# The WKV recurrence of a two-block fp32 model on one core: from one group of heads at a time to two groups in alternation

## Chip, cores and metric

One core of a Trainium2 chip runs the whole program once. The metric is the device time of that execution in microseconds, as the median of several runs.

## What is computed

The reference is two model blocks on 256 tokens of width 2048 in fp32. The first is banded attention, a multi-window pool and a gated feed-forward with a short convolution. The second has an RWKV-7 mixer, then a differential-attention layer. Only the RWKV-7 mixer's recurrence and what surrounds it are touched here:

```
def step(S, inp):
    r_t, w_t, k_t, v_t, kk_t, a_t = inp
    sa = jnp.einsum('bhvk,bhk->bhv', S, kk_t)
    S = (S * w_t[:, :, None, :]
         - sa[..., None] * (kk_t * a_t)[:, :, None, :]
         + v_t[..., None] * k_t[:, :, None, :])
    y = jnp.einsum('bhvk,bhk->bhv', S, r_t)
    return S, y
...
mu = jnp.mean(y, -1, keepdims=True)
yc = y - mu
var = jnp.mean(yc * yc, -1, keepdims=True)
y = (yc * lax.rsqrt(var + GN_EPS)).reshape(B, T, C) * gn_g + gn_b
...
y = (y + bonus.reshape(B, T, C)).astype(x.dtype)
return (y * jax.nn.silu(g)) @ w_out
```

There are 32 heads of 64 channels. y is normed per head ("head norm"), gets a bonus term, is gated, and is multiplied with the output weights (the out-projection).

## The kernel before

All engines are programmed by hand: each has its own function with its instructions in fixed order, and semaphores between them. No scheduler moves anything, so the text of each engine's function is its queue.

Large products. Every weight matrix comes in units of 4 x 128 rows by 256 columns. SP loads a unit (raw_w), ACT rounds it (w_hi), DVE subtracts (w_lo, `split_unit`, L2448), and PE multiplies both parts with the activations. The out-projection begins with `first_body` (L931, L934): 8 units, each in two halves, in four depths x. Depth x needs the k-tiles of head group x as rounded operand (`operand_hi`, ACT) and rest (`operand_lo`, DVE); the gates are counts of `gn_ready`, 4 per group.

The recurrence. The 256 tokens are cut into 4 chunks (c = 0 to 3) of 64, the 16 tiles of heads into 4 groups (g = 0 to 3) of 4 tiles, 8 heads each. The order is `STEPS = [(g, c) for g in range(4) for c in range(NCH)]`: 16 steps, all chunks of a group and then the next group. PE's function `step(n)` issues, in this order:

- `x_second`: the state's part of x (c > 0), `k_pairs(n + 1)`: products of k with r and kappa of the next step
- first u product: inverse blocks times x; `turn_v(n + 1)`
- cross product, `beta_pairs(n + 1)`, state times r into y (c > 0), second u product
- `turn_k(n + 1)`, state sums (c < 3), `turn_beta(n + 1)`, `x_first(n + 1)`, y product

All these products are small: `quads` (L1319) issues eight of 64 columns into quarters of the array. Between them ACT copies x, the first u, half of u, v and k/beta out of PSUM, and y into its place; DVE masks the pairs (`read_kappa` L3037, `read_rho` L3043), adds the cross product to x (L3057), copies the other half of u (L3063) and moves the state (L3075, L3077, L3081). POOL squares y (L866), multiplies the bonus (L849) and gates (`by_gate`, L854). SP loads for each step its inverse and cross blocks (`load_t`), three steps deep, and spreads the rows of 1/std over partitions through DRAM (`spread_rows`).

The head norm of group g-1 runs in the steps of group g: squares summed on PE (`group_squares`, L1423) in its first step, variance and reciprocal (L3060, L3096) on DVE, square root on ACT, spread by DMA, and `head_pair` (L3108, L3113) on DVE for two tiles at a time. Only group 3 is left for after the loop: `head_squares` (L1430) after unit 0 of `first_body` and `last_rows_wide` (L1439) after unit 3, which spreads the rows by products into PSUM. Weight units 0 to 3 of the out-projection are split within the steps 6, 10, 14, 14 (ACT) and 10, 14, 15, 15 (DVE), by `SPLIT_AT` and `LOW_SPLIT_AT`; at step 15 DVE does them after its copy of u and `operand_lo(0)`.

Of the kernel before, what the change touches and what calls it, by code (L numbers as in the profile page):

```python
# [14 lines left out]
P = 128  # L15
T = 256
# [130 lines left out]
def program(nc, h):  # L147
# [14 lines left out]
    with root:  # L162
# [95 lines left out]
        with ExitStack() as s1:  # L258
# [8 lines left out]
            with ExitStack() as s2:  # L267
# [7 lines left out]
                with ExitStack() as s3:  # L275
                    HTP = sb(s3, "xs_pair", [P, 2, T])
# [3 lines left out]
                    with ExitStack() as s4:  # L280
                        TB = sb(s4, "inverse_blocks", [P, 3, 4, CHUNK])
                        S = sb(s4, "wkv_s", [P, 4, CHUNK])
# [17 lines left out]
            with ExitStack() as s2:  # L300
# [4 lines left out]
                with ExitStack() as s3:  # L305
                    SMALL = sb(s3, "wkv_small", [P, 2, 8, T])
                with ExitStack() as s3:
                    sb(s3, "place_of_small", [P, 2, 8, T])
                    GSQ = sb(s3, "group_norm_squares", [P, 4, T])
                    GROWS = sb(s3, "head_rstd_rows", [P, 2, T])  # L310
                    GWIDE = sb(s3, "head_rstd_wide", [P, 4, T])
                with ExitStack() as s3:
                    sb(s3, "place_of_half_b", [P, KD, T])
                    HT3B = sb(s3, "xs_quarter_b", [P, 4, T])
# [86 lines left out]
        l_ready, ones_ready, decays = sem("log_decay"), sem("decay_ones"), sem("decays_ready")  # L401
# [4 lines left out]
        inv_in, blanked = sem("lt_loaded"), sem("blocks_blanked")  # L406
# [8 lines left out]
        x_done, xs_ready, u_done, us_ready = sem("wkv_x_done"), sem("wkv_x_ready"), sem("wkv_u_done"), sem("wkv_u_ready")  # L415
# [10 lines left out]
        dist_in, lam_prod, lam_sum, lam_exp = sem("dist_and_ln_rows_loaded"), sem("lam_products"), sem("lam_sum"), sem("lam_exp")  # L426
# [112 lines left out]
        def k_kappa(m):  # L539

            return SMALL[:, m, 0, :].rearrange("p (i c) -> p i c", i=4)

        def with_rho(m):

            return SMALL[:, m, 1:3, :].rearrange("p h (i t) -> p h i t", i=4)

        def v_and_u(m):

            return SMALL[:, m, 3:5, :].rearrange("p a b -> p (a b)").rearrange("p (j e h t) -> p j e h t", j=2, e=2, h=2)

        def k_and_beta(m):

            return SMALL[:, m, 5:7, :].rearrange("p a b -> p (a b)")

        def k_beta_turned(n):

            g, c = STEPS[n]
            return 3 * g + min(c, 2) + 1

        def v_turned(n):  # L560

            return n + 1 + (k_beta_turned(n - 1) if n else 0)
# [4 lines left out]
        v_bank = lambda n: V_BANK if n else SIDE[:, 1, T:]  # L567
        kb_bank = lambda n: KB_BANK if n else SIDE[:, 3, :]

        def by_two(x):  # L570

            return x.rearrange("p e (j t) -> p e j t", j=2)
        SPLIT_AT = [6, 10, 14, 14]
# [2870 lines left out]
```

## Time and profile before

| | us |
|---|---|
| median of 3 runs | 2164.82 |
| lowest, highest | 2163.67, 2165.35 |
| span of the profiled execution | 2162.8 |
| of it, first product of the loop to the last y product | 1467.31 to 1562.63 |

The span runs from the first to the last instruction; the runs' times also hold what lies around it, and the difference of the profiled span to the median is 2.0 us. The trace has a start and a duration for each instruction. Groups of matmuls are shown as one row with their count; each fp32 product counts as two. A start is measured, an end modelled, so lengths of small products are read from start to start.

### The profile page before, as it was taken

Reading aid. Unit: us, or ns where it says so; the run is one execution under the profiler, and the core shown is the slowest. Engines: PE = TensorE matmul, PEld = TensorE weight load, DVE = VectorE, ACT = ScalarE, POOL = GpSimd, SP = SyncE. Lnnn points to the kernel's source line nnn. Section 1 sums busy time; section 2 is a strip of 40 time slices with the busy share of each in tenths; the row PEclk is TensorE's granted clock in tenths of the full one; section 3 lists DMA queues with packets and bytes.
Section 4 is the critical chain, followed back from the end, with each engine's and each line's share of the span. In section 5 each row is a group of like instructions: output and inputs, shape, how many; then the busy total and the mean of one; then the engine's idle time right before and its main releaser. Section 6 shows DMA issues by size and latency. Waiting matters only on the chain.

```text
span 2162.8 us, 36139 instructions
## 1 busy us (share of the span) xinstructions
PE 2128.1 (98%) x13990; PEld 1808.1 (84%) x13990; DVE 1466.9 (68%) x2083; ACT 1063.6 (49%) x1516; POOL 85.8 (4%) x75
## 2 busy tenths in 40 slices
PE   9999999999999999999899999999899999999998
PEld 7888878888888888888788888887788888888886
DVE  6556568885478855786795599884776544567656
ACT  5444455444444433444644766544434534456543
POOL 0800000000000000000000000001211000000000
PEclk9999999999999999999999999999999999999999
DMA  9654545555656556555465656653454555654553
GB/s 299 202 165 157 172 160 185 190 186 189 198 185 190 187 187 199 187 180 177 150 203 167 196 183 179 206 160 86 129 174 142 185 185 195 186 155 146 173 197 117
DMA packets 398856, 384.43 MB, mean 178 GB/s; under 512 B 43660, under 2 KB 395460, under 8 KB 397764
## 3 DMA queue, kind: packets, MB, share of 16 engines
q1 hardware_dynamic: 398728, 382.66, 55.8%
q8 instruction: 88, 1.44, 0.3%
q14 instruction: 40, 0.33, 0.1%
HBM read 375.73 MB, written 6.87 MB: 177 GB/s over the span
## 4 chain that ended last, share of the span: by engine, by line
PE 89%; DVE 7%; issue 2%; ACT 1%; DMA 1%; POOL 0%; SPq 0%; DVEq 0%; ACTq 0%; POOLq 0%
PE acc L894 35%; PE acc L897 17%; PE acc L1020 5%; PE acc L1022 5%; PE acc L1021 5%; PE acc L931 3%; PE acc L986 2%; PE acc L987 2%; PE acc L988 2%; PE aux L1319 2%; PE acc L934 1%; DVE w_lo L3001 1%; PE acc L1619 1%; PE acc L1620 1%; PE acc L1621 1%
## 5 line engine op out<-in xcount | busy, mean ns | idle before, releaser
L2448 DVE TENSOR_TENSOR w_lo<-raw_w,w_hi 128x1024 fp32r<-128x1024 f32 (+1 forms) x570 | 683.5, 1224 | 438.3 <-ACT w_hi L1692 437.5
L1692 ACT ACTIVATE w_hi<-raw_w 128x1024 fp32r<-128x1024 f32 (+1 forms) x570 | 586.3, 1045 | 706.0 <-PE acc L897 413.0
L894 PE MATMUL acc<-h,w_hi 128*128 128x512 f32 x1664 | 525.8, 397 | 0.0
L897 PEld LDWEIGHTS acc<-h,w_lo 128*128 128x128 f32 x1664 | 312.6, 188 | 73.8
L897 PE MATMUL acc<-h,w_lo 128*128 128x256 f32 x1664 | 327.0, 278 | 0.0
L894 PEld LDWEIGHTS acc<-h,w_hi 128*128 128x128 f32 x1664 | 254.7, 189 | 1.0
L894 PE MATMUL acc<-x_split,w_hi 128*128 128x512 f32 x704 | 225.1, 401 | 0.0
L894 PE MATMUL acc<-xs_b,w_hi 128*128 128x512 f32 x512 | 162.0, 398 | 1.0 <-DVE w_lo L3001 0.9
L897 PEld LDWEIGHTS acc<-x_split,w_lo 128*128 128x128 f32 x704 | 132.2, 188 | 31.2
L3001 DVE TENSOR_TENSOR w_lo<-raw_w,w_hi 128x1024 fp32r<-128x1024 f32 x96 | 116.8, 1219 | 42.1 <-ACT w_hi L2165 41.2
L894 PE MATMUL acc<-xs_a,w_hi 128*128 128x512 f32 x448 | 142.3, 399 | 0.7 <-DVE w_lo L3001 0.7
L897 PE MATMUL acc<-x_split,w_lo 128*128 128x256 f32 x704 | 138.7, 278 | 0.0
L1020 PE MATMUL acc<-w_hi,ff 128*128 128x512 f32 x346 | 135.2, 391 | 2.9 <-DVE w_lo L2448 2.9
L1021 PE MATMUL acc<-w_lo,ff 128*128 128x512 f32 x352 | 137.5, 391 | 0.0
L1022 PE MATMUL acc<-w_hi,ff 128*128 128x512 f32 x346 | 135.1, 390 | 0.0
L2165 ACT ACTIVATE w_hi<-raw_w 128x1024 fp32r<-128x1024 f32 x96 | 100.8, 1054 | 53.2 <-PE acc L897 45.6
L897 PEld LDWEIGHTS acc<-xs_b,w_lo 128*128 128x128 f32 x512 | 96.2, 188 | 22.7
L894 PEld LDWEIGHTS acc<-x_split,w_hi 128*128 128x128 f32 x704 | 108.1, 189 | 2.4 <-issue 0.8
L897 PEld LDWEIGHTS acc<-xs_a,w_lo 128*128 128x128 f32 x448 | 84.2, 188 | 20.0
L897 PE MATMUL acc<-xs_b,w_lo 128*128 128x256 f32 x512 | 100.6, 278 | 0.0
L897 PE MATMUL acc<-xs_a,w_lo 128*128 128x256 f32 x448 | 88.1, 278 | 0.0
L894 PEld LDWEIGHTS acc<-xs_b,w_hi 128*128 128x128 f32 x512 | 78.0, 189 | 3.4 <-issue 1.6
(459 smaller groups left out, 3223.5 us busy)
## 6 DMA issues: line engine op xcount, KB each, us to landing
raw_w<-in_w_up SPq DMA_DIRECT2D x172, 512.0 KB, 3.5
raw_w<-in_a_w_in SPq DMA_DIRECT2D x124, 512.0 KB, 3.9
raw_w<-in_w_in SPq DMA_DIRECT2D x64, 512.0 KB, 3.9
raw_w<-in_w_down SPq DMA_DIRECT2D x64, 512.0 KB, 3.5
raw_w<-in_b_w_qg SPq DMA_DIRECT2D x64, 512.0 KB, 3.7
raw_w<-in_w_o SPq DMA_DIRECT2D x32, 512.0 KB, 3.5
raw_w<-in_a_w_out SPq DMA_DIRECT2D x32, 512.0 KB, 3.5
raw_w<-in_w_k_shared SPq DMA_DIRECT2D x32, 512.0 KB, 3.3
```

The source lines that it names most:

```text
L894: pe.matmul(ACC[2 * b + f], WHI[:, q if hi is None else hi, k, f * P:(f + 1) * P], op[:, kt, :, :].rearrange("p h t -> p (h t)"), start=fi ...
L897: mm = pe.matmul(ACC[2 * b + f][:, 0:T], WLO[:, slot, k, f * P:(f + 1) * P], op[:, kt, 0, :], start=False, stop=last)
L931: pe.matmul(ACC[2 * b + f], hi(2 * x + b)[:, k, f * P:(f + 1) * P], op[:, kt, :, :].rearrange("p h t -> p (h t)"), start=first, stop=False)
L986: pe.matmul(out, xh, wh[:, :, k, :], start=(kt == 0), stop=False)
L987: pe.matmul(out, xh, wl[:, :, k, :], start=False, stop=False)
L1020: pe.matmul(out[t_], xh, wh, start=(x + k == 0), stop=False)
L1021: pe.matmul(out[t_], xh, wl, start=False, stop=False)
L1022: mm = pe.matmul(out[t_], xl, wh, start=False, stop=(x == 3 and k == ku - 1))
L1692: act.activation(WHI[:, u % 4, 0:ku, :], RAWW[:, u, 0:ku, :], ACT.Copy).then_inc(hi_made, 1)
L2165: act.activation(WHI[:, n % 4, :, :], RAWW[:, slot, :, :], ACT.Copy).then_inc(hi_made, 1)
L2448: dve.tensor_tensor(WLO[:, u, 0:ku, :], RAWW[:, u, 0:ku, :], WHI[:, u % 4, 0:ku, :].bitcast(F32), ALU.subtract)\
L3001: dve.tensor_tensor(WLO[:, slot_of(n), :, :], RAWW[:, slot_of(n), :, :], WHI[:, n % 4, :, :].bitcast(F32), ALU.subtract)\
```

## The change

The step order becomes pairs of groups: (0,0) (1,0) (0,1) (1,1) and so on, then groups 2 and 3. A loop of 17 periods replaces the 16 steps. Period n begins step n (x, first u, cross) and ends step n-1 (second u, state sums, y). State, x and u have an even and an odd buffer, v/u three. Each engine's queue is written anew in this order. The head norm of groups 0 and 1 runs in periods 8 to 16, by the new tables; groups 2 and 3 are squared and summed behind the last step. SP's block loads wait for `u_done` instead of `y_done`. Some semaphores are merged.

```
-        STEPS = [(g, c) for g in range(4) for c in range(NCH)]
+        STEPS = [(2 * pair + q, c) for pair in range(2) for c in range(NCH) for q in range(2)]
+        X_AT, U_AT, W_AT = (0, P), (T, 384), (T, 384)
+        ROWS_AT, ROOT_AT, PAIR_OUT_AT, GATES_AT = {8: 0, 9: 1}, {9: 0, 12: 1}, {12: 0, 13: 1, 15: 2, 16: 3}, {12: 0, 13: 1}
...
             for n in range(3, 4 * NCH):
-                sp.wait_ge(y_done, n - 2)
+                sp.wait_ge(u_done, n - 2)
...
-                if n >= 7 and n % 4 == 3:
-                    spread_rows(n // 4 - 1)
+                if n in (12, 15):
+                    spread_rows((n - 12) // 3)
...
-            def last_rows_wide():
+            def rows_wide(g):
 
-                pe.wait_ge(gn_rstd, 4)
+                pe.wait_ge(gn_rstd, g + 1)
+                pe.wait_ge(gn_read, 4)
+                if g == 2:
+                    pe.wait_ge(y_out, len(STEPS))
+                else:
+                    pe.wait_ge(gn_out, 6)
...
+            def period(n):
+                begun, ending, next_ = n < len(STEPS), n > 0, n + 1 < len(STEPS)
+                if begun and STEPS[n][1] > 0:
+                    x_second(n)
+                if next_:
+                    turn_v(n + 1)
+                    k_pairs(n + 1)
+                if ending:
+                    u_second(n - 1)
+                    y_first(n - 1)
+                if next_:
+                    beta_pairs(n + 1)
+                if ending:
+                    state_sums(n - 1)
+                if begun:
+                    u_first(n)
+                if ending:
+                    y_second(n - 1)
+                if next_ and STEPS[n + 1][1] < 3:
                     turn_k(n + 1)
...
+                    turn_beta(n + 1)
+                if next_:
                     x_first(n + 1)
...
+                if begun:
+                    cross(n)
+                if n in (8, 9):
+                    group_squares(n - 8)
...
-                                                     after={0: lambda: head_squares(AUX[1][:, 0:T], 3), 3: last_rows_wide}), L4)
+                                                     after={0: lambda: rows_wide(2), 3: lambda: rows_wide(3)},
+                                                     halfway=lambda: head_squares(AUX[0][:, T:], 3)), L4)
```

`head_squares(AUX[0][:, 0:T], 2)` stands between the loop and `first_body`. ACT's period copies x, v of the next step, u, the first u, y, then k/beta. DVE's:

```
+            def period(n):
+                next_ = n + 1 < len(STEPS)
+                if next_:
                     read_kappa(n + 1)
...
+                if n:
+                    u_copy(n - 1)
+                if next_:
+                    read_rho(n + 1)
+                if n and STEPS[n - 1][1] < 3:
+                    state_moved(n - 1)
+                if n < len(STEPS):
+                    x_less_cross(n)
+                if n in ROWS_AT:
...
+                    head_reciprocal(g)
+                if n == len(STEPS):
+                    head_variance(AUX[0][:, 0:T], 2)
+                if n in PAIR_OUT_AT:
+                    spread_pair(PAIR_OUT_AT[n])
                 for u in heads_at(n, LOW_SPLIT_AT):
                     split_unit(u)
...
+                if n == 15:
+                    operand_lo(0)
```

The turns have the same operands before and after; of `turn_v` only the start and stop flags differ:

```
-                for i in range(4):
-                    b = i % 2
-                    mm = pe.matmul(v_bank(n)[64 * b:64 * b + 64, i // 2 * P:(i // 2 + 1) * P], tile_of(V, n, i), CENTRE, start=(i < 2), stop=(i >= 2))
...
+                for i in range(4):
+                    at_, b = (i // 2 * P, i % 2) if half is None else (i * P, half ^ i % 2)
+                    mm = pe.matmul(bank[64 * b:64 * b + 64, at_:at_ + P], x[:, 4 * g + i, c * CHUNK:(c + 1) * CHUNK], by, start=True, stop=True)
```

DVE's queue at the end of the loop, before, from the last x less cross (wkv_x) to the out-projection's operands (wkv_out is the rounded rest of y, w_lo a weight unit, the copy into wkv_small half of u):

```order
L3057 TENSOR_TENSOR wkv_x<-aux,wkv_x 128x256 [waits wkv_w_done]
L3063 COPY wkv_small<-aux 64x2x2x64 [waits wkv_u_done]
L3049 TENSOR_TENSOR wkv_out<-beta,wkv_out 128x4x256 [waits gn_hi]
L2448 TENSOR_TENSOR w_lo<-raw_w,w_hi 128x1024 [waits hi_made] x2
L3049 TENSOR_TENSOR wkv_out<-beta,wkv_out 128x4x256 [waits gn_hi]
```

And now:

```order
L3134 TENSOR_TENSOR wkv_x_odd<-aux,wkv_x_odd 128x256 [waits wkv_w_done]
L3186 SCALAR_TENSOR_TENSOR beta<-beta,params,head_rstd_wide 128x256 [waits bonus_done,gn_wide_loaded]
L3186 SCALAR_TENSOR_TENSOR beta<-beta,params,head_rstd_wide 128x256
L3191 SCALAR_TENSOR_TENSOR beta<-beta,params,bonus 128x256 [waits dve_step]
L3191 SCALAR_TENSOR_TENSOR beta<-beta,params,bonus 128x256
L2506 TENSOR_TENSOR w_lo<-raw_w,w_hi 128x1024 [waits hi_made] x2
L3107 TENSOR_TENSOR wkv_out<-beta,wkv_out 128x4x256 [waits gn_hi]
L3111 COPY wkv_small<-aux 64x2x2x64 [waits wkv_u_done]
L3178 TENSOR_SCALAR head_rstd_rows<-aux 128x256 [waits gn_sq_sum]
L3174 RECIPROCAL head_rstd_rows<-head_rstd_rows 128x256 [waits gn_sums_read]
```

The copy of the last u has moved behind a spread pair, two weight units and the operand of group 0.

PE's queue where the out-projection begins, now (group_norm_squares is the sum of squares of group 3; head_rstd_rows the spread of group 2):

```order
L1446 MATMUL aux<-group_norm_squares,consts 32x256 x3
L941 MATMUL acc<-wkv_out,w_hi 128x512 [waits gn_ready]
L941 MATMUL acc<-wkv_out,w_hi 128x512
L944 MATMUL acc<-wkv_out,w_lo 128x256 x2
L941 MATMUL acc<-wkv_out,w_hi 128x512 x2
L944 MATMUL acc<-wkv_out,w_lo 128x256 x2
L1460 MATMUL aux<-head_rstd_rows,consts 64x256 [waits wkv_y_out,gn_sums_read,gn_rstd]
L1460 MATMUL aux<-head_rstd_rows,consts 64x256 x7
```

The spread of group 2's rows, with its wait for DVE's reads of both groups' sums, now stands after three half units; before, the rows of the last group alone were spread, after eight.

## Rows read from the trace of the kernel before

**Rows 1.** The page, part 1: busy us (share of the span) x instructions of each engine.

```profile
PE 2128.1 (98%) x13990; PEld 1808.1 (84%) x13990; DVE 1466.9 (68%) x2083; ACT 1063.6 (49%) x1516; POOL 85.8 (4%) x75
```

**Rows 2.** Timeline of PE where the loop begins: start, us, instruction, idle before it.

```profile
1467.31 0.67 PE L1376 MATMUL acc<-r_kappa,k 64*64 64x128 f32 x16
...
1468.95 0.66 PE L1401 MATMUL acc<-consts,x 128*64 128x128 f32 x8 [0.74 <-DVE silu_g L2526]
```

**Rows 3.** Timeline of PE: pieces of a full step, and of a short one.

```profile
1473.62 0.46 PE L1319 MATMUL aux<-wkv_s,r_kappa 64*64 64x64 f32 x16
1473.90 0.62 PE L1376 MATMUL acc<-r_kappa,k 64*64 64x128 f32 x16
1474.68 0.46 PE L1319 MATMUL aux<-wkv_x,inverse_blocks 64*64 64x64 f32 x16 [0.16 <-ACT wkv_x L2234]
1475.07 0.66 PE L1401 MATMUL acc<-consts,x 128*64 128x128 f32 x8
1475.66 0.46 PE L1319 MATMUL aux<-wkv_u,cross_blocks 64*64 64x64 f32 x16
...
1477.68 0.69 PE L1319 MATMUL acc<-wkv_small 128*64 128x64 f32 x16
...
1479.74 0.46 PE L1319 MATMUL aux<-wkv_s,r_kappa 64*64 64x64 f32 x16
...
1483.80 0.69 PE L1319 MATMUL acc<-wkv_small 128*64 128x64 f32 x16 [0.55 <-DVE wkv_small L3063]
```

**Rows 4.** Groups by line, 1465 to 1565: busy us, mean ns of one, idle before.

```profile
L3043 DVE TENSOR_TENSOR wkv_small<-acc,consts 128x512 f32<-128x512 f32 x15 | 10.4, 691 | 0.5
...
L3037 DVE TENSOR_TENSOR wkv_small<-acc,consts 128x256 f32<-128x256 f32 x15 | 6.3, 421 | 8.5 <-PE acc L1376 8.5
...
L3096 DVE RECIPROCAL head_rstd_rows<-head_rstd_rows 128x256 f32<-128x256 f32 x3 | 5.3, 1754 | 0.4 <-DVE wkv_s L3081 0.2
...
L854 POOL TENSOR_TENSOR beta<-beta,silu_g 128x512 f32<-128x512 f32 x4 | 5.1, 1278 | 9.3 <-DVE beta L3113 9.3
...
L3113 DVE SCALAR_TENSOR_TENSOR beta<-beta,params,bonus 128x256 f32<-128x256 f32 x8 | 3.5, 481 | 0.1
...
L2229 ACT ACTIVATE wkv_out<-beta 128x1024 fp32r<-128x1024 f32 x2 | 2.1, 1049 | 0.0
...
L2253 ACT ACT_TABLE_LOAD x1 | 1.3, 1283 | 0.0
...
L3049 DVE TENSOR_TENSOR wkv_out<-beta,wkv_out 128x1024 fp32r<-128x1024 f32 x1 | 1.2, 1226 | 0.0
```

**Rows 5.** Timeline of all engines at the loop's end.

```profile
1558.29 1.22 DVE L2448 TENSOR_TENSOR w_lo<-raw_w,w_hi 128x1024 fp32r<-128x1024 f32 x1
...
1560.61 0.46 PE L1319 MATMUL aux<-wkv_u,cross_blocks 64*64 64x64 f32 x16 [0.47 <-ACT wkv_u L2240]
...
1561.13 0.42 DVE L3057 TENSOR_TENSOR wkv_x<-aux,wkv_x 128x256 f32<-128x256 f32 x1 [1.63 <-PE aux L1319]
...
1562.14 0.43 DVE L3063 COPY wkv_small<-aux 64x256 f32<-64x256 f32 x1 [0.58 <-PE aux L1319]
...
1562.63 0.69 PE L1319 MATMUL aux<-wkv_small 128*64 128x64 f32 x16 [0.55 <-DVE wkv_small L3063]
...
1563.88 0.74 PE L931 MATMUL acc<-wkv_out,w_hi 128*128 128x512 f32 x2 [0.57 <-DVE wkv_out L3049]
```

**Rows 6.** Timeline of all engines in the out-projection's first body.

```profile
1568.28 0.64 PE L1430 MATMUL aux<-group_norm_squares,consts 128*32 128x256 f32 x8
...
1569.28 1.92 DVE L3108 SCALAR_TENSOR_TENSOR beta<-beta,params,head_rstd_wide 128x256 f32<-128x256 f32 x2
...
1576.02 0.69 PE L1439 MATMUL aux<-head_rstd_rows,consts 32*64 32x256 f32 x16
...
1586.33 0.73 PE L931 MATMUL acc<-wkv_out,w_hi 128*128 128x512 f32 x2
```

**Rows 7.** Busy time of PE behind the first body, with granted clock and DMA share.

```profile
1590.50:1620.00 29.50, 29.50 (x176) 1.00 0.58 184
```

More of the change, by code:

```diff
@@ L913, in tiles_of, with first_body @@
                 return [(sem_, base + 1)] + [(sem_, base + p_ + 2) for p_ in range(1, 8)], (sem_, base + 2)
[L915 removed]
+            def first_body(op, gates, after={}, halfway=None, second=None, depth=(0, 1, 2, 3), hi=lambda u: WHI[:, u % 4], lo=lambda u: WLO[:, u]):
                 for x, q in enumerate(depth):
@@ L935, in first_body @@
                                                start=False, stop=last)
+                        if halfway is not None and (x, pr, b) == (0, 0, 1):
+                            halfway()
                         if pr == 1:
@@ L1452, in x_second @@
             def x_second(n):
-                g, c = STEPS[n]
-                pe.wait_ge(x_begun, 3 * g + c)
-                pe.wait_ge(s_ready, 3 * g + c)
-                quads(XU_BANKS, 0, at(KAP, n), state, between, False, True).then_inc(x_done, 1)
-            def step(n):
-                g, c = STEPS[n]
-                m = n % 2
-                more = n + 1 < len(STEPS)
-                state_next = more and STEPS[n + 1][1] < 3
-                inverse, cross = block_of(TB[:, n % 3, :, :]), far(CRS[:, n % 3, :, :])
-                if c > 0:
-                    x_second(n)
-                if more:
-                    k_pairs(n + 1)
+                pe.wait_ge(x_begun, later_to(n))
@@ L1468, in step, with u_first @@
+                pe.wait_ge(s_ready, sums_to(n - 2))
+                quads(XU_BANKS, X_AT[n % 2], at(KAP, n), state(n), between, False, True).then_inc(x_done, 1)
+            def u_first(n):
                 pe.wait_ge(t_loaded[n % 3], 96 * (n // 3 + 1))
                 pe.wait_ge(xs_ready, n + 1)
-                quads(XU_BANKS, P, inverse, mid(XS), across, True, True).then_inc(u_done, 1)
-                if more:
-                    turn_v(n + 1)
-                pe.wait_ge(us_ready, 3 * n + 1)
@@ L1474, in step, with cross @@
-                quads(XU_BANKS, T, cross, far(US), between, True, True).then_inc(w_done, 1)
-                if c == 0 and g:
-                    group_squares(g - 1)
-                if more:
-                    beta_pairs(n + 1)
+                if n:
+                    pe.wait_ge(u_ready, 2 * n)
+                quads(XU_BANKS, U_AT[n % 2], block_of(TB[:, n % 3, :, :]), mid(XX[n % 2]), across, True, True).then_inc(us_done, 1)
+            def cross(n):
+                pe.wait_ge(us_ready, n + 1)
```

341 lines of the change are left out of this document (180 added, 161 removed).

## Prediction

> **What bounds the kernel now.** I read the page first: TensorE (PE) is busy for 98% of the span [rows 1], so what PE waits for, or is given to do more, is the time. The busy share hides waits of small products, whose ends are modelled, so the stage that changes is read from the timeline, by starts. The WKV loop begins on PE at 1467.31 [rows 2] and its last cross product starts at 1560.61 [rows 5]: 93.3 us. A full step (c=1) takes 6.12 us from 1473.62 to 1479.74, of which only about 0.35 is waiting, before the first u product at 1474.68 [rows 3]; a step whose successor needs no turns of k and beta takes 5.8 with about 1.35 of waiting, 0.73 of it before 1483.80, where PE waits for u to come back from DVE [rows 3]. Counted like this over the loop, start to start less the products' own issue times: first step 1.36; c=0 0.40 and twice 1.26 (the later ones wait for POOL's squares); c=1 three times 0.35 and once 1.37; c=2 5.5 together; c=3 three times 0.39; the last 1.4. That is 14.8. **So the chain costs at most 15 us of the 93.3, and the other 78.5 are issue**, which alternation cannot touch. Behind the loop, the out-projection's first body starts at 1563.88 [rows 5] and ends at 1590.5 (its last gate opens at 1586.33, then three half units of 1.40 [rows 6]); from 1590.5 on PE does not wait [rows 7], so whatever is lost or won before passes to the end.
>
> **The turns.** The words of the change say that v, k and beta are now turned by whole tiles. The operands are the same 128x64 tiles and 128 columns in both, four products each; priced at 0.
>
> **The loop, worked from the rows.** The number of products per step stays. Pieces by start-to-start: 64-row group 0.28, or 0.39 where a full-height group follows (1473.62, 1474.68); v turn 0.59 (1475.07 to 1475.66) [rows 3]. Written in the new order, a full period holds about 5.6 of issue against 5.77 before. One squares' sum of 0.57 [rows 6] leaves the loop. Work before the last cross: 78.5 - 0.6 - 1.3 = 76.6 (the 1.3 is 0.17 in each of the eight periods that have all parts).
> The recurrence now has two periods. State sums begin 2.6 into a period, DVE ends the state at 4.3, and the product that wants it starts at 5.7. So the chain's own waits go, as meant. What is late next is DVE's queue. PE's beta pairs need read_kappa: k pairs start at 1.0, DVE can read at 1.7 and is done at 2.1 (0.42 [rows 4]), just when PE arrives; then u_copy (0.43), for which state sums wait. But x_less_cross now stands at DVE's period end, with PE's cross product last: it ends 0.7 into the next period. Whatever DVE does behind it has only 1.0 us of cover:
> - the reciprocal (0.43 + 1.75 [rows 4]) in periods 8 and 9, behind a squares' sum that is itself the last product: 1.6 + 1.3;
> - spread pairs (four operations of 0.48, 1.8 in a row [rows 4]) in periods 12 and 13: with the short period's wait for y 1.27 each, 2.5;
> - the table load of 1.28 [rows 4] on ACT in period 2, now ahead of x and u copies that PE wants early: 0.9;
> - entry: turn_v(1) is now the first product and waits for DVE until 1468.95 [rows 2], where before k pairs and the first u product filled it: 1.64, and 0.7 + 0.9 + 0.6 for lack of a partner in periods 0 to 2;
> - small ones: 0.1 in each full period, 0.5 in periods 5 and 6 (cross waits for y), 0.2 in 7 and 8, 0.5 in 11 (weight splits): 2.2;
> - period 15, chain bare and behind ACT's two splits: 2.9.
> Sum 15.2. The last cross starts 76.6 + 15.2 = 91.8 after the loop's start instead of 93.3: **-1.5 us**. Cover named: SP's block loads now wait for u_done two periods back and have over 7 us of slack; the row spreads land a period early.
>
> **From the last cross product (C) to the out-projection.** Before: DVE ends x less cross at C+0.94 (1561.13), u is copied (1562.14), y starts at 1562.63, first body at C+3.27 [rows 5]. Now period 15 on DVE goes on with spread pair 2 (1.8), two low splits (1.22 each [rows 5], 2.45), and the low operand of group 0 (1.23 [rows 4]), and only period 16 begins with u_copy(15): C + 0.94 + 1.8 + 2.45 + 1.23 = C+6.4, copy 0.43, y at C+6.9 and 0.6 long, squares' sum 0.57: first body at C+8.1. **+4.8 us.** Queued behind this copy is all of PE.
>
> **The first body.** Its 16 half units are 1.40 each, 22.4; before it took 26.6. Now groups 2 and 3 are both normed behind the loop. PE: two halves and the squares of group 3 to C+11.5, a third half to C+12.9, then rows_wide(2), which waits for gn_read 4, DVE's first operation for group 3. DVE gets there late: variance of group 2 to 10.4; pair 3 to 12.2; then, ahead of group 3, operand_lo(1), which needs POOL's gate (1.28 [rows 4]) to 13.5, ACT's split 4 (free only when unit 0 is done, 13.0) to 14.1 and hi(1) (1.05 [rows 4]) to 15.15; lo(1) to 16.45, then the read at 16.9. **Stall 4.1.** PE: rows to 17.5, half 18.9, depth 1 to 24.5, rows_wide(3) to 25.05. DVE: reciprocal to 18.7, pairs 4 and 5 to 23.3 (one with POOL beside it takes 1.92 + 0.88 instead of 1.8 [rows 6]), split 24.5, pair 6 can only follow rows_wide(3): 27.0, lo(2) 28.3. **Stall 3.25.** Depth 2 to 33.9, depth 3 with its gate at 35.45 to C+39.65. First body 31.55 against 26.6: **+4.95 us** (before lost 4.2 over the halves' 22.4: the squares at 1568.28 and the rows at 1576.02 [rows 6], and the waits beside them).
>
> **Sum.** -1.5 + 4.8 + 4.95 = +8.25. The profiled execution's span is 2162.8 and the median of the runs 2164.82; the 2.0 around the span stays. Forecast 2164.82 + 8.25 = **2173.1 us**. Bounds: the loop's waits lie between what period 15 and the entry must cost (5, -10 more) and 3 more than worked out; the two late parts between +6 and +13.
>
> **A rule beside the rows.** With a gate of POOL beside them, two of DVE's pair operations took 1.92 [rows 6], where two of 0.48 [rows 4] issued back to back would take 0.96 or less. The Trainium skill (SBUF — State Buffer, Who interferes with whom) says that a DVE instruction with two SBUF inputs and a GpSimd one that reads SBUF exclude each other: whoever comes second waits for the whole of the first. By that rule, every one of gates 4 to 7 could cost DVE its full length. The trace agrees in size (1.0 more, for a gate of 1.28 [rows 4]). By the rule alone the sum would be as in rival 3.
>
> **Rivals.**
> 1. *The alternation pays in full (faster).* DVE's load in a period with a pair is 3.2 + 1.8 = 5.0, less than the 5.7 of PE. If its lateness is absorbed within the period (deciding point: DVE's addition behind x_less_cross under 1.0 us more than I count), the waits of periods 2 to 14 go: the 15.2 of waits shrink to some 5: -1.5 - 10.2 = -11.7. Then u_copy +4.8, and with an earlier hi(1) only one of the two stalls, +2.4: -4.5, 2160.3. Against: the order of DVE's instructions is fixed, and kappa and u stand behind the long ones. 0.14.
> 2. *Half of it (no change).* Loop -6, tail +7.5: -6 + 7.5 = +1.5, 2166.3. DVE may be ahead of my hand count. 0.16.
> 3. *DVE and POOL exclude each other in the norm of two groups.* Gates beside pairs and splits on the path three times, 1.3 each: +3.9, 2177.0. 0.17.
> 4. *The turns are cheaper (the change does what its words say).* Nothing in the operands says so; under 0.01.
> Forecast's own case: 0.53.
>
> **The numbers.** A measurement of this kernel tells about 0.2%, 4.3 us, from no change. Faster than 2160.5: most of rival 1 and a little of 2, 0.13. Within 4.3: 0.15. Slower: the forecast, rival 3, the rest of 2: 0.72. Range: from rival 1's edge to above rival 3, 2161 to 2178; the forecast's own case is 2168 to 2176.
>
> **What would show it.** Right: full periods of 5.6 to 5.8 with almost no wait; PE waiting before beta pairs or state sums in periods 9, 10, 13, 14; 4 to 5 us between the last u product and y, with DVE's splits in between; PE idle before rows_wide(2) and before depth 2, released by DVE. Wrong: a last cross product earlier than 85 us after the loop's start; a first body under 29 us; or a wait for SP's block loads, which I put at none.

## The result, and the profile after

| | before | after |
|---|---|---|
| median, us | 2165.09 (2163.67 to 2165.76) | 2192.97 (2188.60 to 2198.56, 4 runs) |
| ratio of after to before, 95% interval | | 1.0134 [1.0122, 1.0146] |
| span of the profiled execution | 2162.8 | 2191.5 |
| first `turn_v` to last cross product | 91.66 | 103.00 |
| last cross product to first body | 3.27 | 8.64 |
| first body | 26.74 | 36.34 |
| end of the first body to the end of the span | 572.2 | 574.55 |

The kernel became 28 us slower, not 8. The four pieces take up the whole difference of the spans, 28.7: 11.3 in the loop, 5.4 between loop and out-projection, 9.6 in the first body, 2.35 behind it. I count from the first row of `turn_v` here (1468.95 before [rows 2], 1468.97 now), since both kernels have it.

PE's and DVE's shares are within a point of those before [rows 1]; the page's first part shows nothing of the loss, only PE's 10 us more of busy time for 8 more recorded instructions:

```profile
PE 2138.4 (98%) x13998; PEld 1818.4 (83%) x13998; DVE 1471.0 (67%) x2083; ACT 1067.5 (49%) x1516; POOL 85.6 (4%) x75
```

PE's timeline in the changed kernel: the loop's start, an early period from state product to state product, and later ones. They answer to [rows 2] and [rows 3].

```profile
1468.97 0.66 PE L1413 MATMUL acc<-consts,x 128*64 128x128 f32 x8 [1.48 <-DVE silu_g L2584]
...
1478.38 0.46 PE L1331 MATMUL aux<-wkv_s,r_kappa 64*64 64x64 f32 x16
...
1480.67 0.46 PE L1400 MATMUL acc<-r_kappa,beta 64*64 64x64 f32 x16 [0.41 <-DVE wkv_small L3095]
...
1484.10 0.92 PE L1331 MATMUL aux<-wkv_s_odd,r_kappa 64*64 64x64 f32 x16
...
1507.06 0.46 PE L1331 MATMUL aux<-wkv_s,r_kappa 64*64 64x64 f32 x16 [0.71 <-DVE wkv_s L3123]
...
1515.58 0.46 PE L1331 MATMUL aux<-wkv_s_odd,r_kappa 64*64 64x64 f32 x16 [2.81 <-DVE wkv_s_odd L3123]
```

The early period takes 5.72 us, 0.41 of it waiting, and the forecast had 5.6 to 5.8. It is not yet a full one: it has no product of state and r into y, since the step that ends in it has c=0. But the product that wants the state waits for it in later periods, which the forecast had excluded. The waits of PE in the loop, 1465 to 1575 (total, times, longest), put this first:

```profile
PE aux L1331 <- DVE wkv_s_odd L3123: 6.1, 4, 2.8
PE acc L1400 <- DVE wkv_small L3095: 4.7, 7, 1.2
```

What DVE does then stands in the timeline of all engines before 1515.58:

```profile
1511.05 1.13 PE L1331 MATMUL aux<-wkv_small 128*64 128x64 f32 x32
...
1511.86 0.69 DVE L3101 TENSOR_TENSOR wkv_small<-acc,consts 128x512 f32<-128x512 f32 x1 [2.20 <-PE aux L1331]
...
1512.46 0.41 DVE L3121 TENSOR_TENSOR wkv_s_odd<-acc,wkv_s_odd 128x256 f32<-128x256 f32 x1
...
1512.82 2.34 POOL L861 TENSOR_TENSOR bonus<-bonus,x 128x1024 f32<-128x1024 f32 x1
1512.91 2.53 DVE L3123 TENSOR_TENSOR wkv_s_odd<-wkv_s_odd,chunk_decay 128x256 f32<-128x256 f32 x1
```

Two things are to be seen. `read_rho` (L3101) stands idle for 2.20 us on PE's y product (the x32 row holds y and the `x_first` behind it), and `state_moved` (L3121, L3123) stands behind it, although its sums started at 1509.71, before y. The wait is for the y product of two steps before the one whose pairs are read; in the kernel before it had long been issued when `read_rho` came to it, and the order on DVE was the same. And the state's multiplication takes 2.53 us where it takes 0.43 elsewhere (1506.48), exactly while POOL's bonus product of 2.34 runs. The same pair stands at 1496.78 and 1496.87.

The third part of the loss is the clock. Windows of 5 us in the loop and of 4 around the out-projection's start; the columns are PE, PEld, DVE, ACT, POOL busy with instruction counts, PE's granted clock, DMA share, GB/s:

```profile
1500.00:1505.00 5.00, 5.00 (x118) 4.47 (x118) 0.85 (x2) 1.76 (x5) 0.00 (x0) 0.66 0.18 50
...
1515.00:1520.00 5.00, 4.42 (x118) 4.09 (x119) 1.62 (x4) 1.91 (x5) 0.16 (x1) 0.71 0.12 35
...
1576.00:1580.00 4.00, 1.46 (x20) 1.14 (x24) 2.45 (x3) 0.29 (x1) 0.00 (x0) 0.50 0.00 0
...
1592.00:1596.00 4.00, 4.00 (x15) 3.43 (x14) 3.93 (x9) 1.48 (x2) 1.57 (x2) 0.55 0.08 14
```

Ahead of the first two windows PE had waited 2.35 and 2.81 us for the state, between 1568 and 1592 4.64 and 3.86. Behind each of these the granted clock is at the lower of its two levels, 1.2 GHz, for part of the next windows, so PE works at half speed just when it could catch up. In the kernel before, every window from 1480 to 1640 has 1.00. The length of a wait alone does not decide it. The clock also fell behind two short waits (0.71 and 0.59 at 1567.21 and 1568.26; 0.57 in the window from 1568 to 1572), and it stayed at 1.00 behind the 3.02 us before depth 2 (window from 1604 to 1608).

The end of the loop and the first body, timeline of all engines, to be read against [rows 5] and [rows 6]:

```profile
1571.97 0.46 PE L1331 MATMUL aux<-wkv_u_odd,cross_blocks 64*64 64x64 f32 x16 [0.58 <-ACT beta L2249]
...
1574.54 2.35 DVE L2506 TENSOR_TENSOR w_lo<-raw_w,w_hi 128x1024 fp32r<-128x1024 f32 x2
1576.81 1.22 DVE L3107 TENSOR_TENSOR wkv_out<-beta,wkv_out 128x1024 fp32r<-128x1024 f32 x1
1578.06 0.43 DVE L3111 COPY wkv_small<-aux 64x256 f32<-64x256 f32 x1
...
1578.54 1.12 PE L1331 MATMUL aux<-wkv_small 128*64 128x64 f32 x16 [4.64 <-DVE wkv_small L3111]
1579.59 1.08 PE L1446 MATMUL aux<-group_norm_squares,consts 128*32 128x256 f32 x8
...
1588.64 1.23 DVE L3107 TENSOR_TENSOR wkv_out<-beta,wkv_out 128x1024 fp32r<-128x1024 f32 x1 [4.07 <-ACT wkv_out L2273]
1589.78 0.42 DVE L3178 TENSOR_SCALAR head_rstd_rows_last<-aux 128x256 f32<-128x256 f32 x1
...
1590.30 1.16 PE L1460 MATMUL aux<-head_rstd_rows,consts 32*64 32x256 f32 x16 [3.86 <-issue]
...
1603.06 2.20 POOL L866 TENSOR_TENSOR beta<-beta,silu_g 128x512 f32<-128x512 f32 x1 [5.14 <-DVE beta L3191]
1604.03 2.31 DVE L2506 TENSOR_TENSOR w_lo<-raw_w,w_hi 128x1024 fp32r<-128x1024 f32 x1
1604.17 0.74 PE L941 MATMUL acc<-wkv_out,w_hi 128*128 128x512 f32 x2 [3.02 <-DVE wkv_out L3107]
...
1606.40 0.72 PE L941 MATMUL acc<-wkv_out,w_hi 128*128 128x512 f32 x2 [0.54 <-DVE w_lo L2506]
```

This part went as worked out: the copy of u behind a pair, two splits and the low operand, y at C+6.57 (forecast C+6.9), a stall of 3.86 before the rows of group 2 (4.1), one of 3.02 before depth 2 (3.25). What is longer are products between: the squares' sum of group 2 ahead of the first body and the rows in it take 1.08 and 1.16, where such ones took 0.64 and 0.69 before [rows 6]. And in depth 2 a weight split takes 2.31, beside a gate of POOL, where one takes 1.22 [rows 5]; PE waits 0.54 for it.

### The profile page after: what moved, and what is told of

Its sections match the earlier page's. It is cut to its first block, busy times and chain, and to the rows that moved or that the text cites. A ratio compares the mean times of both kernels' runs of the same rounds, so it can differ in the third digit from the quotient of the medians.

```text
span 2191.5 us, 36203 instructions
## 1 busy us (share of the span) xinstructions
PE 2138.4 (98%) x13998; PEld 1818.4 (83%) x13998; DVE 1471.0 (67%) x2083; ACT 1067.5 (49%) x1516; POOL 85.6 (4%) x75
## 4 chain that ended last, share of the span: by engine, by line
PE 89%; DVE 7%; issue 2%; ACT 1%; DMA 0%; DVEq 0%; SPq 0%; ACTq 0%
PE acc L904 35%; PE acc L907 17%; PE acc L1032 5%; PE acc L1034 5%; PE acc L1033 5%; PE acc L941 4%; PE acc L998 2%; PE acc L1000 2%; PE acc L999 2%; PE acc L944 2%; PE aux L1331 2%; DVE w_lo L3059 1%; PE acc L1663 1%; PE acc L1664 1%; PE acc L1665 1%
```

## The experiments

Nine kernels. The first four are each the changed kernel with one edit. In the table, C is the last cross product of the loop, and "behind" is from the first body's end to the span's end. The pieces are of one profiled execution each, the medians of all runs; beside the experiments the kernel before had medians of 2163.2 to 2163.9, and the ratios are to those.

| kernel | turn_v to C | C to body | body | behind | median, us | ratio to before, 95% |
|---|---|---|---|---|---|---|
| before | 91.66 | 3.27 | 26.74 | 572.2 | 2165.09 | |
| after | 103.00 | 8.64 | 36.34 | 574.55 | 2192.97 | 1.0134 [1.0122, 1.0146] |
| state first | 92.77 | 8.63 | 37.10 | 572.2 | 2181.73 | 1.0078 [1.0057, 1.0099] |
| bonus early | 95.68 | 8.63 | 36.77 | 572.5 | 2183.87 | 1.0099 [1.0082, 1.0116] |
| u copy first | 103.01 | 3.26 | 39.36 | 572.4 | 2186.96 | 1.0107 [1.0090, 1.0124] |
| clock kept | 105.21 | 7.75 | 33.83 | 572.1 | 2186.68 | 1.0104 [1.0087, 1.0121] |
| norm order | 101.24 | 8.88 | 32.36 | 573.5 | 2184.58 | 1.0098 [1.0081, 1.0114] |
| all four edits | 92.08 | 3.27 | 35.32 | 572.7 | 2174.35 | 1.0051 [1.0034, 1.0068] |
| first redrawn order | 100.85 | 4.79 | 29.81 | 574.4 | 2177.46 | 1.0058 [1.0045, 1.0072] |
| second redrawn order | 93.11 | 3.27 | 31.30 | 574.9 | 2170.94 | 1.0031 [1.0019, 1.0042] |
| u copy last, in the kernel before | 91.48 | 5.93 | 27.92 | 574.5 | 2169.28 | 1.0026 [1.0016, 1.0036] |

### The state moved before rho is read

```diff
-                if next_:
-                    read_rho(n + 1)
                 if n and STEPS[n - 1][1] < 3:
                     state_moved(n - 1)
+                if next_:
+                    read_rho(n + 1)
```

> The changed kernel, but DVE moves the state before it masks the next step's output pairs (read_rho), which has to wait for the y product two steps back. Theory Q (queue order: DVE's order and POOL beside it make PE wait for the state): the waits before the state products (2.35, 2.81, three of 0.7, three of 0.24 us) vanish, and with them the half clock behind the two long ones (about 1.5 us each): 8 to 11 us faster than the changed kernel, 2182 to 2185. Rival S (the state's wait is set by the chain y product, pairs, and DVE's two state operations merely stand near it): under 1 us. Rival C (the clock alone, the gaps come anyway): under 2 us.

Measured 2181.73 us, 11.2 less, just past the 8 to 11 that the theory gave. No wait of PE for the state is left in the loop, and the loop is 10.2 us shorter. DVE ends the state 4.4 us into the period (1490.44 to 1494.82), where the forecast had 4.3. DVE's multiplication of the state no longer meets the bonus product either (none of them takes 1 us), so this edit takes away two causes at once, and the next one is needed to tell them apart. Beside the loop, the trace has 2.3 us won behind the first body, where nothing differs, and 0.8 lost in it, where the clock now falls behind the wait before depth 2 too (0.65 from 1596 to 1600). In the granted clock the loop's halved stretches are gone; the one behind its end is not:

```profile
1494.40 0.42 DVE L3123 TENSOR_TENSOR wkv_s_odd<-wkv_s_odd,chunk_decay 128x256 f32<-128x256 f32 x1
```

```profile
1500.00:1525.00 25.00, 22.16 (x676) 18.82 (x676) 12.36 (x24) 11.82 (x29) 7.39 (x7) 1.00 0.34 86
1565.00:1580.00 15.00, 9.27 (x56) 6.73 (x56) 7.20 (x11) 2.80 (x4) 3.14 (x3) 0.67 0.09 31
```

### The bonus product ahead of the squares

POOL waits for `ws_ready`, and multiplies the bonus before it squares y instead of behind it, so that it falls elsewhere in the period. DVE's order is left as in the change.

```diff
+                if n in (3, 5, 7, 9):
+                    pool.wait_ge(ws_ready, n + 1)
+                    times_v((n - 3) // 2)
                 pool.wait_ge(y_out, n + 1)
                 pool.tensor_tensor(GSQ[...], y4, y4, ALU.mult).then_inc(gn_sq, 1)
-                if n in (3, 5, 7, 9):
-                    times_v((n - 3) // 2)
```

> The changed kernel, but POOL's four bonus products (2.34 us each) start when x less cross is done, not behind the squares of y. Theory Q: the state operation of 0.42 us that took 2.53 us beside them, twice, is 0.42 us again: waits before the state products in periods 3 and 5 fall from 2.35 and 2.81 to 0.3 and 0.7, and the half clock behind them goes: 6 to 8 us faster, 2185 to 2187. Rival S (no port, the long operation is a wait of its own): the 2.53 us stay, no change.

Measured 2183.87 us, 9.1 less, more than the 6 to 8 of theory Q; the trace has 2.1 us won behind the first body too and 3.0 ahead of the loop, where nothing differs. No operation of DVE on the state takes 1 us here, and the loop is 7.3 us shorter. Waits of PE in this kernel, 1465 to 1575:

```profile
PE acc L1401 <- DVE wkv_small L3096: 3.4, 5, 1.2
PE aux L1332 <- DVE wkv_s_odd L3124: 1.9, 4, 0.7
...
PE aux L1332 <- DVE wkv_s L3124: 1.4, 3, 0.7
```

What is left of the waits for the state, 1.9 + 1.4 = 3.3 with none over 0.7, is the order alone. It agrees with the 2.9 by which the loop of the experiment before is shorter still (95.68 - 92.77). So of the changed kernel's loop, 7.3 us were POOL's two bonus products beside DVE (2.1 each on DVE, 4.2) and what they drew after them, the halved clock above all (this kernel's loop has 1.00), and 2.9 the place of `read_rho`.

### The copy of u first

```diff
                 if n:
                     u_copy(n - 1)
+                if n == len(STEPS):
+                    operand_lo(0)
+                    spread_pair(2)
+                    split_unit(2)
+                    split_unit(3)
```

(pair 2, splits 2 and 3 and low operand 0 leave period 15.)

> The changed kernel, but DVE copies the last u before spread pair 2, weight units 2 and 3 and the low operand of group 0. The wait of 4.64 us before the last y product falls to 0.6 and the half clock behind it goes (1.5 us). Theory Q (a chain of waits: DVE idles 2.3 and 4.1 us behind it): only about 2 us come back as a longer wait before the rows' spread: 3 to 5 us faster, 2188 to 2190. Rival D (DVE's work behind the loop is the bound): all of it comes back before the rows' spread, within 1 us of the changed kernel.

Measured 2186.96 us, 6 less, where theory Q had 3 to 5. The first body starts 3.26 us behind C, as before the change. But part of the win comes back in the body, which is 3.0 longer, since the variance of group 2 now comes later on DVE and the squares of group 3 wait for it. Two splits of weights stand ahead of that variance and take 3.42 together, beside a gate of POOL of 2.17, where two took 2.35 (1574.54 in the changed kernel). So the pieces give this edit 2.4 (5.4 less 3.0); the rest of the 6 lies behind the body, 2.1, and ahead of the loop, 1.5, where no instruction differs.

```profile
1575.64 3.42 DVE L2506 TENSOR_TENSOR w_lo<-raw_w,w_hi 128x1024 fp32r<-128x1024 f32 x2
1575.80 2.17 POOL L866 TENSOR_TENSOR beta<-beta,silu_g 128x512 f32<-128x512 f32 x1 [1.28 <-DVE beta L3194]
...
1579.66 0.64 PE L1446 MATMUL aux<-group_norm_squares,consts 128*32 128x256 f32 x8 [2.87 <-DVE head_rstd_rows L3181]
...
1587.12 1.26 PE L1460 MATMUL aux<-head_rstd_rows,consts 32*64 32x256 f32 x16 [3.98 <-issue]
```

### The clock kept up

Products whose results nobody reads fill the two longest gaps, 8 before y and 7 before the rows of group 2. They take nothing off the chain.

```diff
+                if n == len(STEPS) - 1:
+                    pe.wait_ge(rest_out, n + 1)
+                    keep_clock_at(ACC[0][:, 0:T], 8)
...
+                if g == 2:
+                    keep_clock_at(AUX[1][:, 0:T], 7)
                 pe.wait_ge(gn_rstd, g + 1)
```

> The changed kernel with fifteen products more, whose results nobody reads: eight before the wait for the last u copy, seven before the wait for the rows' spread. They fill about 3.4 and 3.0 us of gaps of 4.6 and 3.9 us. Theory C (gaps lower the granted clock, and 3 to 4 us of products behind each then run at half): the clock behind both gaps stays at 1.0, 3 to 4 us faster, 2189 to 2190. Rival: the clock falls for another reason, no change or slower by what the products add (0 to 1 us).

Measured 2186.68 us: with the useless work added the kernel was 6 us faster, where theory C had 3 to 4. Of that, 0.9 between loop and body and 2.5 in the body stand where the fillers are. The windows beside those of the changed kernel (there 0.50 to 0.76 between 1576 and 1584, 0.55 to 0.60 between 1588 and 1596):

```profile
1500.00:1525.00 25.00, 21.13 (x564) 18.50 (x567) 10.19 (x18) 9.80 (x24) 4.13 (x4) 0.80 0.23 59
1565.00:1580.00 15.00, 10.66 (x242) 8.69 (x235) 9.37 (x16) 5.45 (x10) 1.88 (x3) 1.00 0.52 177
1580.00:1600.00 20.00, 17.71 (x142) 13.63 (x139) 13.16 (x22) 6.29 (x8) 6.65 (x5) 1.00 0.25 82
```

The clock is 1.00 at both fillers, and still 0.80 in 1500 to 1525, where there are none. It also falls behind the wait of 3.02 before depth 2, which has no filler (0.71 from 1604 to 1608). The 105.21 of the loop in this run is 2.2 more than in the changed kernel, with the same instructions in the loop; 1.5 of it is the loop's entry. There PE waits 1.48 and 0.55 in every kernel with alternation, and takes 9.41 from `turn_v` to the first state product in six of them, with the clock at 1.00; it takes 10.9 here, 10.93 with all four edits and 10.80 in the first redrawn order, with the clock at 0.70 to 0.75 from 1468 to 1472. So the same wait is followed by the low clock in one execution and not in another, and a loop compared between two executions carries up to 1.5 us of this.

### The order in the head norm

```diff
-            operand_lo(1)
             head_variance(AUX[0][:, T:], 3)
+            operand_lo(1)
...
-            split_unit(4)
             operand_hi(1)
+            split_unit(4)
```

> The change with two pairs of neighbours swapped behind the last step: VectorE makes the variance of group 3 before the low operand of group 1, and ScalarE the high operand of group 1 before the split of unit 4. In the changed kernel VectorE stands 4.07 us before that low operand, the variance of group 3 and its reciprocal behind it, and TensorE then waits 3.86 us before the first spread of rows at 1590.3 and again 3.02 before depth 2. Theory N (the order of the two engines in the head norm makes both waits): the wait before the spread of rows (2) nearly goes, the granted clock stays at 1.00 between 1586 and 1596 because the gap that lowered it is gone, the wait before depth 2 shrinks by 1 to 3 us, the first body ends 4 to 6 us earlier, and the kernel takes 2187 to 2189 us against 2193. Rival P (the port: VectorE and GpSimd exclude each other on gates, pairs and splits, so what is not waited for at one place is waited for at the next): the stall moves to depth 2 or 3 and the end moves by less than 1.5 us.

Measured 2184.58 us, a little more than theory N gave. The stall before the rows of group 2 is gone, that before depth 2 stays at 3.02, so N had that wrong; behind it the clock is at 0.52 (1596 to 1600), where the changed kernel had 1.00. The body is 4.0 shorter; the rest of the gain comes from the loop of this run, which is 1.8 shorter, from behind the body, 1.1, and from ahead of the loop, 1.9, with nothing changed in any of them.

```profile
1583.20 0.69 PE L1460 MATMUL aux<-head_rstd_rows,consts 32*64 32x256 f32 x16
...
1594.69 0.73 PE L941 MATMUL acc<-wkv_out,w_hi 128*128 128x512 f32 x2 [3.02 <-DVE wkv_out L3107]
```

### The reverse, in the kernel before

If the late copy of u costs what it seems to, the kernel before must lose time when it gets one (not shown: the splits and the low operand leave their old places behind the copy):

```diff
+                if not more:
+                    split_unit(2)
+                    split_unit(3)
+                    operand_lo(0)
                 dve.wait_ge(u_done, 2 * n + 2)
                 dve.tensor_copy(v_and_u(n % 2)[64:P, ...], ...)
```

> The kernel before, with one thing taken over from the change: VectorE copies the last step's u behind two low splits and the low operand of group 0 instead of ahead of them. In the kernel before that copy starts at 1562.14 and the first body 3.27 us behind the last cross product. Theory Q (what stands ahead of the copy delays the y product, the first body, and through the gap the granted clock): the copy comes 3 us later, the first body starts about 6.4 us behind the last cross product, and the kernel takes 2167 to 2170 us against 2164: 3.1 for the copy, and up to 2 more if the gap lowers the clock to 0.5 or 0.6 for some us. Rival H (the first body would have stood later for split low parts and the rows of the norm anyway, so the delay is taken up there): under 1 us, 2164 to 2165, and no lower clock.

Measured 2169.28 us, in the range of theory Q, with an interval that lies above 1. Timeline of PE and the window around it:

```profile
1564.45 1.12 PE L1319 MATMUL aux<-wkv_small 128*64 128x64 f32 x16 [3.40 <-DVE wkv_small L3067]
1565.51 1.22 PE L931 MATMUL acc<-wkv_out,w_hi 128*128 128x512 f32 x2
```

```profile
1564.00:1568.00 4.00, 3.55 (x23) 3.05 (x24) 1.34 (x2) 1.33 (x2) 0.61 (x1) 0.50 0.42 180
```

A gap of 3.4 us, and y and the first product take 1.12 and 1.22 instead of 0.69 and 0.74 [rows 5]. In the pieces: 2.7 until the body, 1.2 in it, and 2.3 behind it, of which more at the end. So 3.8 of the loss stand where the edit is; the piece up to the body was expected at 6.4 and is 5.93.

### All four edits together

State first, bonus early, u copy first and the order in the norm.

> The change with four edits at once: the state moved before the rho product is read, the bonus product ahead of the squares on GpSimd, the last copy of u ahead of the pair and the splits, and the two swaps in the norm. Alone the first three gave 11, 9 and 6 us (2181.7, 2183.9, 2187.0 against 2193.0). Theory Q (each edit removes waits of its own, and the granted clock stays up where the gaps go): the loop's last cross product comes at 1559 to 1562, the first body starts 3.3 us behind it, lasts 32 to 35 us, and the kernel takes 2171 to 2177 us; still above the 2164 of the kernel before, because the loop is then no shorter than before (93.3 us). Rival O (the first two edits mostly remove the same waits, and what the tail gains is given back behind the first body): 2178 to 2183 us.

Measured 2174.35 us, theory Q. The loop is 92.08 against 91.66 before the change. With the waits for the state gone, a period with every product takes 5.70 us and has no wait; a step with every product took 6.12 before, about 0.35 of it waiting [rows 3]. So such a period wins 0.4 us.

```profile
1490.45 0.46 PE L1332 MATMUL aux<-wkv_s,r_kappa 64*64 64x64 f32 x16
...
1496.15 0.46 PE L1332 MATMUL aux<-wkv_s_odd,r_kappa 64*64 64x64 f32 x16
```

The loop is not free of loss for all that. Waits of PE, 1465 to 1575, and 1.5 us of low clock at the entry:

```profile
PE acc L1401 <- DVE wkv_small L3096: 4.2, 7, 1.2
PE aux L1332 <- ACT wkv_x_odd L2284: 1.9, 2, 1.5
```

What the trace has left of the loss, 8.6 us, is in the first body. There the squares of group 3 wait 2.90 for DVE, behind two splits that again take 3.42 beside a gate (1564.84), and depth 2 waits 3.02 with the low clock behind it (0.70 from 1584 to 1588).

### The norm and the loop drawn up anew

Two kernels with the same work in another order: the low splits, pairs and reciprocals of groups 0 and 1 moved within the loop (the reciprocal of group 0 in two halves), and behind it

```diff
+            operand_lo(0)
+            spread_pair(3)
+            head_variance(AUX[0][:, 0:T], 2)
+            head_reciprocal(2)
+            split_unit(2)
+            head_variance(AUX[0][:, T:], 3)
             operand_lo(1)
-            head_variance(AUX[0][:, T:], 3)
+            split_unit(3)
             wide_pair(4)
             wide_pair(5)
             split_unit(4)
-            wide_pair(6)
+            head_reciprocal(3)
             operand_lo(2)
             split_unit(5)
+            wide_pair(6)
```

(this is the second; in the first, pair 3 is in period 14 and low operand 1 directly behind the reciprocal of group 2).

> The change with its order of work drawn up anew, products and amounts of work unchanged: state moved before rho is read and the bonus product ahead of the squares, as before; the norm of groups 0 and 1 spread over periods 8 to 14 (pairs 0 to 3 at the ends of periods 11 to 14, the reciprocal of group 0 in halves, that of group 1 a period later and in rows of its own), the low splits 0 and 1 in the free stretch of period 15, the high splits 2 and 3 two periods earlier; behind the last step VectorE does low operand 0, variance and reciprocal of group 2, low operand 1, split 2, variance 3, split 3, pairs 4 and 5, split 4, reciprocal 3. Theory Q (what the loop gives is bounded by TensorE's own 5.7 us in a period, and the rest of the loss is order in the norm, each gap of which also halves the clock): the last cross product comes 91 to 92 us after the loop's start, the first body 3.3 us behind it and lasts 27.5 to 30 us, against 93.6, 3.3 and 35.3 in the version with four edits; the kernel takes 2163 to 2167 us, within 0.2% of before on one side or the other. Rival T (two groups' norm behind the last step do not fit beside one body of products, whatever the order, because VectorE's own chain of 21 operations is as long as the stretch): the body still lasts 33 us or more, and the kernel takes 2169 to 2173 us.

Measured 2177.46 us, above both theories. The body came out as said, 29.81 us, but the loop took 100.85 (1.4 of it the low clock at the entry) and the body began 4.79 behind it, not 3.3: I had moved pair 0 to period 11, before its rows were there, and left ScalarE's square root of group 1 waiting for the same rows. The timeline of all engines:

```profile
1543.31 0.88 DVE L3193 SCALAR_TENSOR_TENSOR beta<-beta,params,head_rstd_wide 128x256 f32<-128x256 f32 x2 [2.30 <-DMA head_rstd_wide<-head_rstd_scratch]
1543.37 0.42 ACT L2270 ACTIVATE head_rstd_rows_last<-head_rstd_rows_last 128x256 f32<-128x256 f32 x1 [2.84 <-DMA head_rstd_wide<-head_rstd_scratch]
...
1544.20 0.46 PE L1332 MATMUL aux<-wkv_x_odd,inverse_blocks 64*64 64x64 f32 x16 [2.20 <-ACT wkv_x L2284]
```

> The first redrawn order with its mistakes in the loop taken out: there VectorE waited 2.30 us in period 11 for the wide rows of group 0, ScalarE 2.84 for them before its square root of group 1, and SyncE held the last rows back behind a pair; TensorE lost 2.20, 1.73 and 1.19 us to it and ran at a clock of 0.90 between 1525 and 1560, while the first body lasted 29.8 us. Here pairs 0 and 1 are at the ends of periods 12 and 13 again, pair 2 in the free stretch of period 15, pair 3 behind low operand 0, and the square root of group 1 waits for nothing but its variance. Theory Q: no wait of TensorE in the loop over 1.5 us, the last cross product 91 to 93 us after the loop's start, the first body 3.3 us behind it and 30 to 32 us long, the kernel at 2166 to 2169 us, still 2 to 5 us above the one before, since the loop is bounded by TensorE's own 5.7 us in a period and the body behind it carries a norm of two groups. Rival W (the waits of the loop come back elsewhere, since VectorE has about 1.2 us to spare in a period and a pair takes 1.75): 2172 to 2176 us, as the version with four edits.

Measured 2170.94 us, 1.9 over the expected range, with the pieces of loop and body as expected (93.11, 3.27, 31.30). Against the version with four edits the body gives 4.0, the loop takes 1.0 back, and 2.2 more are lost behind the body. It has the lowest median with alternation here, 22 us below the change, and still 0.31% above the kernel before; its interval overlaps that of the version with four edits.

## Why the prediction was wrong

Slower was right, and the tail was right in its mechanism. The size was wrong: forecast +8.25, measured +28.7 in the spans (+27.9 in the medians), outside the range. By terms (forecast, measured): loop -1.5, +11.3; last cross product to body +4.8, +5.4; first body +4.95, +9.6; behind it 0, +2.35.

- **"State sums begin 2.6 into a period, DVE ends the state at 4.3 ... So the chain's own waits go."** This step failed. It took DVE's time for the state from the end of the sums and left out what stands ahead of it in DVE's own queue: `read_rho(n + 1)`, whose wait for `y_done` is in the diff's context. With a buffer two deep it is the wait for y of step n-1, and the new order issues that y in the same period, behind the state sums. The prediction listed DVE's work behind `x_less_cross` and never its waits in the middle. In a period of the changed kernel with every product, DVE ends the state at 5.9, not 4.3 (1547.99 to 1553.93); with the two swapped it ends it at 4.4. Cost: 2.9 us in the loop by itself, and it put the state's multiplication where POOL's product falls.
- **DVE and POOL.** Rival 3 had the right mechanism, with the price of a gate (1.3), in the norm behind the loop. It struck hardest in the loop, with POOL's bonus product, which the prediction nowhere counts: 2.53 for 0.43 on DVE, twice, on the path both times; with the clock behind it 7.3 us, the largest single error. In the norm it cost less than the 3.9 of the rival: a split of 2.31 and a low operand of 1.78 (0.68 without a gate beside it, 1611.93) each kept PE from a product, 0.54 and about 0.25 us. The rule of the Trainium skill that the prediction cites (SBUF — State Buffer, Who interferes with whom: the one that comes second waits for the whole of the first) is borne out here: DVE came 0.09 behind a product of 2.34 and lost 2.1. The same section names DVE instructions with two inputs in SBUF, and the rows agree: L3123 was hit, with state and decay, while L3121 just before it, which reads the sums from PSUM, took its usual 0.41 (1512.46) with POOL's squares of y beside it, which took their usual 0.61 (1512.25).
- **The clock.** The prediction has no term for it: the granted clock was 1.00 in every row that it read, and it forecast three gaps of 3 to 5 us on PE without asking what PE would run at behind them. In the first body the halved stretches cost 3.0 us against the run with fillers, which has 1.00 there: two half units take 3.59 instead of 2.99 (1580.61 to 1584.20), the rows and five half units 10.17 instead of 7.80 (1590.30 to 1600.47). That is most of the 4.8 by which the body exceeds its forecast of 31.55. Another 1.2 is in depth 2, which takes 6.76 instead of 5.6 (1604.17 to 1610.93): PE waits there for the split beside a gate, and at its end for the operand beside the next one. The rest is mostly that half units behind another product take a little more than the 1.40 of the sum (two take 2.99 there, not 2.80).
- **The loop's other waits.** With the state first, the loop takes 92.77, where the forecast corresponds to 90.2 (91.8 less the 1.64 up to `turn_v`). The 2.6 between them are not shown to come from any one place. The long wait in period 15, 1.47 for ACT's copy of x behind its two splits, was in the forecast, with 2.9 for the whole period. The waits before the beta pairs, which I had at 5.4 behind reciprocals and pairs, are 1.17 and 0.90 behind the reciprocals and 0.42 behind a pair in that kernel; all seven of the loop come to 4.9. The issue of a full period, which I had at 5.6, is 5.70.
- **From the last cross product to the body:** C+8.1 forecast, C+8.64 measured, and with the y product at half speed (1.12 for 0.69). The reverse experiment confirms it. Right.
- **The range** failed with the loop. Its bound for the waits was 3 us above the value worked out, taken from nothing but my own count. Rivals 1 and 2 did not happen, and no edit brought them about: the shortest loop with alternation, 92.08, is no shorter than before. A period with every product wins 0.4 us. That no order of this loop could win more is not shown, since that one still has 6.1 us of waits and 1.5 of low clock at its entry.

The forecast said what would show it wrong: an earlier cross product, a shorter body, a wait for block loads. It named nothing for a longer loop, which is what came.

## What to carry to other kernels

When a chain is rearranged, write down for each engine on it the whole queue between two links, with the wait of every entry; an entry that waits for last step's output, in a buffer two deep, moves with that output and holds all that stands behind it. Ask of each long operation of GpSimd where it will fall against VectorE's short ones on the path. And price a gap of some us on TensorE at more than its length: here four of the five waits of 2.35 to 4.64 us were followed by a stretch at half the clock, which cost 3.0 us in the first body alone.

## What had not been expected of the hardware

- Products without use in two gaps went with a kernel 6 us faster (ratio 1.0104 against 1.0134), with the granted clock at 1.00 where it had been 0.50 to 0.76. 3.4 of it stand in the two pieces with the gaps.
- One and the same wait is not always followed by the low clock. Behind the 3.02 us before depth 2 the changed kernel went on at 1.00 (1604 to 1608), and the five kernels with one edit, which have the same wait, fell (0.52 from 1596 to 1600 in the order in the norm).
- Behind the first body all these kernels run the same instructions, yet from 60 to 100 us behind its end the granted clock has one of three means: 0.96, 0.91 or 0.87. The kernels with 0.96 need 572.1 to 572.7 us to the end, those with 0.91 (the change, the order in the norm, the first redrawn order, u copy last) 573.5 to 574.55, the one with 0.87 (the second redrawn order) 574.9. The windows, of the kernel before and of that one:

```profile
1650.60:1670.60 20.00, 20.00 (x129) 17.86 (x122) 12.93 (x20) 7.53 (x12) 1.99 (x2) 0.92 0.41 132
1670.60:1690.60 20.00, 19.49 (x110) 16.71 (x109) 16.82 (x23) 17.98 (x29) 3.44 (x3) 1.00 0.37 117
```

```profile
1656.40:1676.40 20.00, 20.00 (x122) 18.21 (x114) 10.90 (x17) 6.28 (x9) 0.00 (x0) 0.85 0.41 132
1676.40:1696.40 20.00, 20.00 (x103) 17.17 (x102) 16.63 (x22) 17.32 (x29) 5.44 (x4) 0.90 0.32 104
```

So up to 2.8 us of a difference between two of these kernels can come from a place where they do not differ. Ahead of the loop there is another such place: `turn_v` starts at 1465.96 to 1469.07 in the nine traces with alternation. What decides between the three clock values is left open; with one profiled execution of each kernel it cannot be said whether it belongs to the kernel or to the run.
